# Seven products instead of eight in the last group's down projection, and product 4 of a job issued right behind its product 3

## The reference

```
def half_swiglu(x, g, w_gu, w_down):
    h = rmsnorm(x, g) @ w_gu                    # 1024 -> 2 x 2816
    a, b = jnp.split(h, 2, axis=-1)
    return x + 0.5 * ((jax.nn.silu(a) * b) @ w_down)   # 2816 -> 1024
...
for i in range(DEPTH):                          # DEPTH = 2
    h = half_swiglu(h, norm_ffn_a[i], w_ffn_a_gu[i], w_ffn_a_down[i])
    h = h + mixer(rmsnorm(h, norm_mix[i]))
    h = half_swiglu(h, norm_ffn_b[i], w_ffn_b_gu[i], w_ffn_b_down[i])
    h = h + sigmoid(rmsnorm(h, norm_ple[i]) @ ple_w_gate[i]) * (p[i] @ ple_w_proj[i])
```

## Time and profile before

| | us |
|---|---|
| median of 3 runs | 2784.4 (2784.36 to 2786.01) |
| the profiled execution | 2784.26 |
| its span, first to last instruction | 2782.7 |
| PE busy | 2744.7 (99%) |
| DVE busy | 1920.1 (69%) |
| ACT busy | 1207.2 (43%) |
| POOL busy | 191.7 (7%) |

### The profile page before, as it was taken

One profiled execution on the slowest core, in us unless ns is written; L12 is line 12 of the kernel. 1 busy time (PEld: TensorE's weight loads), 2 busy tenths in 40 slices (PEclk: granted clock), 3 DMA queues, 4 the chain that ended last, 5 costly groups with the idle time before them and its releaser, 6 DMA issues.

```text
span 2782.7 us, 47474 instructions
## 1 busy us (share of the span) xinstructions
PE 2744.7 (99%) x18946; PEld 2699.7 (97%) x18946; DVE 1920.1 (69%) x2691; ACT 1207.2 (43%) x1629; POOL 191.7 (7%) x190
## 2 busy tenths in 40 slices
PE   8999999999999999999999999999999999999997
PEld 8999999999999999999999999999999999999997
DVE  7888864646464678888557788865555568888755
ACT  5445443323132444454444455444534443545443
POOL 0000003101010110000010000002000020000021
PEclk9999999999999999999999999999999999999998
DMA  3322323333232313323321222223222112232231
GB/s 120 95 84 79 97 79 124 110 103 114 92 110 95 104 55 94 87 81 92 93 76 60 85 85 87 88 84 121 88 83 91 68 61 72 77 101 77 86 99 53
DMA packets 80909, 246.96 MB, mean 89 GB/s; under 512 B 8465, under 2 KB 25121, under 8 KB 79681
## 3 DMA queue, kind: packets, MB, share of 16 engines
q1 hardware_dynamic: 71408, 204.67, 23.6%
q0 software_dynamic: 9296, 39.40, 3.9%
HBM read 226.74 MB, written 17.30 MB: 88 GB/s over the span
## 4 chain that ended last, share of the span: by engine, by line
PE 97%; DVE 2%; ACT 0%; issue 0%; DMA 0%; ACTq 0%; SPq 0%; DVEq 0%
PE ps L618 42%; PE ps L547 35%; PE ps L930 7%; PE ps L806 4%; PE ps L983 2%; PE ps L599 1%; PE ps L904 1%; PE ps L1017 1%; PE ps L967 1%; PE ps L871 1%; PE ps L855 0%; PE ps L1003 0%; PE ps L874 0%; PE ps L849 0%; PE ps L883 0%
## 5 line engine op out<-in xcount | busy, mean ns | idle before, releaser
L1086 ACT ACTIVATE w_hi<-raw 128x1024 fp32r<-128x1024 f32 (+2 forms) x210 | 201.3, 959 | 522.4 <-PE ps L547 382.3
L1729 DVE TENSOR_TENSOR w_lo<-raw,w_hi 128x1024 fp32r<-128x1024 f32 (+2 forms) x210 | 238.1, 1134 | 100.5 <-ACT w_hi L1086 97.5
L547 PE MATMUL ps<-x_hi,w_hi 128*128 128x320 f32 x1216 | 283.7, 315 | 9.7 <-DVE x_lo L1734 8.7
L547 PE MATMUL ps<-x_hi,w_lo 128*128 128x320 f32 x1216 | 277.6, 310 | 0.0
L547 PE MATMUL ps<-x_lo,w_hi 128*128 128x320 f32 x1216 | 277.4, 309 | 0.0
L547 PEld LDWEIGHTS ps<-x_hi,w_hi 128*128 128x128 f32 x1216 | 204.3, 188 | 13.5 <-DVE w_lo L2472 8.7
L547 PEld LDWEIGHTS ps<-x_lo,w_hi 128*128 128x128 f32 x1216 | 203.9, 188 | 0.0
L547 PEld LDWEIGHTS ps<-x_hi,w_lo 128*128 128x128 f32 x1216 | 203.7, 188 | 0.0
L1150 ACT ACTIVATE wx_hi<-raw 128x1024 fp32r<-128x1024 f32 (+1 forms) x92 | 92.4, 1004 | 252.4 <-PE ps L618 215.1
L618 PE MATMUL ps<-x_hi,w_hi 128*128 128x320 f32 x576 | 178.7, 310 | 0.0
L618 PE MATMUL ps<-x_hi,w_lo 128*128 128x320 f32 x576 | 177.9, 309 | 0.0
(11 more groups left out here) (310 smaller groups left out, 7714.4 us busy)
## 6 DMA issues: line engine op xcount, KB each, us to landing
raw<-wst SPq DMA_DIRECT2D x292, 512.0 KB, 3.6
raw<-wst SPq DMA_DIRECT2D x96, 384.0 KB, 3.2
raw<-wst SPq DMA_DIRECT2D x32, 256.0 KB, 2.6
s<-st_d POOLq DMA_DIRECT2D x8, 1024.0 KB, 5.1
sts_o<-s POOLq DMA_DIRECT2D x16, 512.0 KB, 3.3
rd<-dec_d POOLq DMA_DIRECT2D x8, 640.0 KB, 5.5
kc<-kc_d POOLq DMA_DIRECT2D x8, 512.0 KB, 4.3
vc<-vc_d POOLq DMA_DIRECT2D x8, 512.0 KB, 5.2
```

The lines of the kernel that those rows point to most:

```text
L547: last = nc.tensor.matmul(out[:, h, :], a, b[:, HALF * h:HALF * (h + 1)], start=start and q == 0, stop=stop and q == 2, skip_group_check=True)
L1086: nc.scalar.activation(w_hi[:, (c["n"] + m) % 2, 0:cols], raw[:, r, 0:cols], ACT.Copy).then_inc(s_whi, 1)
L1729: tt(w_lo[:, p, 0:cols], raw[:, r, 0:cols], w_hi[:, p, 0:cols].bitcast(F), ALU.subtract).then_inc(s_wlo, 1)
```

## The change

Three things are done at once.

1. `SEVEN_DOWN` gets group 3 too: its down projection becomes four dn jobs of seven products. The eight plain units go, `x_hi`, `x_lo` and the squares for the next phase are made two tiles at a time (`fed`, `square_of`), and the squares move to another place in SBUF (`squares`).
2. On PE, product 4 of the old job moves up behind its product 3: 1, 3 old, 4 old, 2, 6, 5, 7.
3. ACT's and DVE's orders in a job follow: `hi12(new)` and `lo12(new)` move behind the finished job's work.

```
-SEVEN_DOWN = (1, 2)
+SEVEN_DOWN = (1, 2, 3)
...
                             third(old)
-                            second().then_inc(s_prod[2], 1)
-                            sixth().then_inc(s_prod[6], 1)
                             if after_start:
                                 split_up_to("T4")
                             fourth(old)
+                            second().then_inc(s_prod[2], 1)
+                            sixth().then_inc(s_prod[6], 1)
                             fifth()
...
-                    with pe.Fori(0, KT // 4) as i:
-                        for j in range(4):
-                            step(m + j, i, 4)
-                            project(c, m + j, i, 4, (c["unit"] + 1 + m + j) % 4, [(k, k) for k in range(nf)],
-                                    tiles(g_hi), tiles(g_lo), ready if j == 0 else None)
...
+                def fed(d):
+
+                    act.wait_ge(s_up, CREDIT + 2 * d["sum"] + 2)
+                    feed_hi(c["norm"] + 1, d["out"])
+                    act.wait_ge(s_free, CREDIT + o + d["m"] + 2)
+                    feed_hi(c["norm"] + 1, d["out"] + 1)
+
+                def square_of(n):
+                    square(c["fed"] + KT, c["norm"] + 1, n, s_xhi, c["fed"] + KT + n + 1)
...
-                        elif new:
-                            hi12(new)
-                        if made and made["seven"]:
+                        if made:
                             silu(made)
-                            snap2(d)
-                        elif old:
-                            snap2(d)
-                            if made:
-                                silu(made)
                         hi34(d)
                         if made:
                             ghi(made)
+                        if old:
+                            if new:
+                                hi12(new)
+                            elif c["split_p"]:
+                                act.wait_ge(s_p, 16 * (c["ple"] + 1))
+                                nc.scalar.activation(p_hi[:], p_raw[:], ACT.Copy).then_inc(s_phi, 1)
+                            snap2(d)
+                        if piece == LAST and d["kind"] == "dn":
+                            fed(old)
+                            square_of(old["out"])
+                            square_of(old["out"] + 1)
...
                         if new:
                             s1_s2(new)
+                        if made:
+                            c12(made)
+                        if new:
                             s3(new)
+                        if made:
+                            gated(made, 1)
+                            if made["seven"] and made["odd"]:
+                                g_sum(made, 1)
+                            gated(made, 0)
+                            if made["seven"]:
+                                g_sum(made, 2)
+                        if new:
                             if old:
                                 lo12(new)
                             else:
                                 lo1(new)
                                 lo2(new)
-                        if made:
-                            c12(made)
-                            gated(made, 1)
...
                             s4(new)
                         lo34(d)
...
                     if piece == LAST:
-                        silu(d)
+                        fed(d)
                         split_hi(c, d["m"] + 1, 0, 0, c["fill"] + d["m"] + 2)
-                        ghi(d)
+                        square_of(d["out"])
+                        square_of(d["out"] + 1)
```

More of the change, by code:

```diff
@@ L254, in trunk @@
         with ExitStack() as s:
+            sb("over_t_hi2", [P, 3, 4, HALF], F, s)
+            sq_mix = sb("sq_mix", [P, 2, TOK], F, s)
+            sb("over_t_mid", [P, 3 * 4 * HALF - 4 * TOK], F, s)
+            sq_ple = sb("sq_ple", [P, 2, TOK], F, s)
+        with ExitStack() as s:
             sb("over_t2", [P, 2, 3, 4, HALF], F, s)
@@ L432, in b_side, with squares @@
             return quarter(whole, *at_x[product]) if product < 5 else extra[:, product - 5, :, :]
+        def squares(norm):
+            if norm == 0 or norm > len(phases) - 1 or phases[norm - 1] != "ffn":
+                return sq
+            return sq_ple if phases[norm] == "ple" else sq_mix
         def g_tile(buf, k):
@@ L1096, in square @@
                 act.wait_ge(s_ssum, CREDIT + c_fed + d - 1)
-                nc.scalar.activation(sq[:, d % 2, :], x[:, d, :], ACT.Square).then_inc(s_sq, 1)
+                nc.scalar.activation(squares(norm)[:, d % 2, :], x[:, d, :], ACT.Square).then_inc(s_sq, 1)
             def feed(c_fed, norm, d, s, value):
@@ L1312, in ffn @@
                     for d in range(KT):
-                        if nf_at < LAST and d >= KT - 2:
+                        if d >= KT - 2:
                             if d == KT - 2:
@@ L1598, in add_squares @@
                         pool.wait_ge(s_ss, CREDIT + norm)
-                        nc.gpsimd.tensor_copy(ssum[:], sq[:, 0, :]).then_inc(s_ssum, 1)
+                        nc.gpsimd.tensor_copy(ssum[:], squares(norm)[:, 0, :]).then_inc(s_ssum, 1)
                     else:
                         pool.wait_ge(s_ssum, CREDIT + fed + d)
-                        nc.gpsimd.tensor_tensor(ssum[:], ssum[:], sq[:, d % 2, :], ALU.add).then_inc(s_ssum, 1)
+                        nc.gpsimd.tensor_tensor(ssum[:], ssum[:], squares(norm)[:, d % 2, :], ALU.add).then_inc(s_ssum, 1)
             def ffn(c):
@@ L1963, in winograd @@
                             c11_c12(summed)
-                            s1_s2(new)
-                            s3(new)
                             c21(summed)
-                            lo12(new)
-                            s4(new)
+                            if new:
+                                s1_s2(new)
+                                s3(new)
+                                lo12(new)
+                                s4(new)
+                            elif c["split_p"]:
+                                dve.wait_ge(s_phi, CREDIT + c["ple"] + 1)
+                                tt(p_lo[:], p_raw[:], p_hi[:].bitcast(F), ALU.subtract).then_inc(s_plo, 1)
                             lo34(d)
+                            if piece == LAST and d["kind"] == "dn":
+                                feed_lo(c["fed"] + KT, c["norm"] + 1, summed["out"])
+                                feed_lo(c["fed"] + KT, c["norm"] + 1, summed["out"] + 1)
                             continue
@@ L1997, in winograd @@
                         split_lo(c, d["m"], 0, 0)
-                        c12(d)
-                        gated(d, 1)
-                        gated(d, 0)
+                        c11_c12(d)
+                        c21(d)
+                        feed_lo(c["fed"] + KT, c["norm"] + 1, d["out"])
+                        feed_lo(c["fed"] + KT, c["norm"] + 1, d["out"] + 1)
                         split_lo(c, d["m"] + 1, 0, 0)
-                        glo(d)
                 for nf_at, nf in enumerate(PIECES):
@@ L2062, in ffn @@
                             t_low((6, 1, 2, 3, 4)[d], 3 + d)
[L2063 to L2068, removed]
+                        if d == KT - 4:
                             first = fast_pairs(c, nf_at + 1)[0]
```

13 lines of the change are left out of this document (3 added, 10 removed).

## The result

The changed kernel took 2827.5 us (median of 4; 2823.8 to 2829.5) beside 2784.4 before: 1.0151 of it, with a 95% interval of 1.0136 to 1.0167, or **43 us more**. I had forecast +20 with a range that ended at 2822. The direction was right, the size was not.

The account below looks back on a forecast made before the run. PE, busy 99% of the span, was taken to bound the kernel, so only fewer matmuls or new gaps count. From 2784.3, -21.1 + 30.8 + 0.7 + 9.4 = +19.8 gave 2804 us, range 2785 to 2822.

Parts of the forecast that it names:

- The saving: Group 3's down projection: 252 matmuls in place of 288, 5.28 us less in each of four FFNs, -21.1 us.
- The ring: Fast groups' gu jobs: DVE's cycle of freeing a raw slot, loading and splitting outlasts PE's job, PE waits, +30.8 us.
- The even turn: Gu jobs, even finished job: s1 to next s1 takes 12.54 us, 0.22 over PE's job.
- The odd turn: Gu jobs, odd finished job: s1 to next s1 takes 13.76 us, 1.44 over PE's job, including 3.82 for the load.
- The final group's own jobs: Group 3's dn jobs: DVE's 9.2 us of work fits PE's 9.24, nothing taken, 1 us a group as bad end.
- The tail: Behind each FFN: two tiles end together, so PE waits for ssum in ple, ret and sb, +9.4 us (0 to 15).
- the first dn job: Final group: the 0.16 us wait at the first dn job comes once more in each FFN, +0.7 us.
- the rivals: Cycle fits PE's job: 2773, 11%; loads sooner: 2785, 8%; loads later: 2820, 10%; change not doing what it says: excluded.
- Loads land later, or the dn jobs of group 3 become DVE's: Rival: loads take 4.08 us or more, 47 for 30.8, giving 2820, or DVE bounds group 3's dn jobs, 2824; 10%.

Follow-up runs that it names:

- after_lo34: The changed kernel with DVE's lo34(d) moved ahead of lo12(new) and s4(new) in gu jobs behind a gu job: 2795.8 us, 1.0042 of before.
- seven_only: The kernel before with only group 3's seven products added; product order and ACT's and DVE's gu orders as before: 2798.6 us, 1.0053 of before.
- adds_later: The changed kernel, but POOL waits for both x_lo of a pair (first three pairs) before it adds the squares: 2819.6 us.

## Why the prediction was wrong

**The saving** of 21.1 us was right, by the count of matmuls.

**The ring** was right in size: its term was +30.8, and undoing it in the changed kernel gave back 31.7. In mechanism it was half right. The even turn was 12.26 for 12.54, by a load that took 3.57 there in place of 3.82. The odd turn came out at 13.76 to the hundredth, and that is luck: no load is waited for in it, and what closes it is DVE's own work behind `lo34`, which stood in no hop of mine and happens to be 3.85 us long.

**The final group's own jobs** is the step that failed: "By their widths DVE has some 9.2 us of work against PE's 9.24: I take nothing". The work was 9.17, but the third job took 12.75, since POOL's two additions in a row fell on it. I had taken the addition's 2.05 us as the whole price of POOL and DVE meeting, which is POOL's side of it. What DVE pays did not stand in the sum: before, each FFN tile had one addition in 5.28 us, beside a DVE that was idle for 2.6 of them, and the `x_lo` there started first and took 0.88. The rule that I named for the tail, from the Trainium skill, "SBUF — State Buffer", section "SBUF: two separate sides" (whichever of a DVE instruction with two SBUF inputs and a GpSimd instruction starts first has the shared ports for its whole length), the trace bears out: two `x_lo` take 4.27 us for 1.68 behind the start of an addition, an `x_lo` that starts ahead of one keeps its 0.88, and with an input from PSUM `c22` keeps its 0.48. I had applied it to the tail alone, and there it was said to add nothing.

**The tail** I had at +9.4, from waits of 3.2 in each `ple` and 1.5 in `ret` and `sb`. (The pieces that I listed add up to 8.9 us and not 8.5; with 8.9 the term would have been 11.0.) The rows give 2.8 in each `ple`, 1.3 in `ret`, and in `sb` a wait of 2.2 for `c21` (L1902), 1.3 more than before, in place of one for `ssum`: 8.2. The waits were right in size; what I lacked is the clock at 0.50 to 0.67 behind the long ones, in the tail and in the final group.

Counted in both traces from the start of one matmul of PE to the start of another, in us for all four FFNs:

| part | forecast | before | changed | difference |
|---|---|---|---|---|
| groups 1 to 3, their first 2016 matmuls in each FFN | +30.8 | 1185.6 | 1217.2 | +31.6 |
| final group's down projection, 288 matmuls, then 252 | -21.1 + 0.7 | 170.0 | 171.7 | +1.7 |
| the 200 matmuls behind it | +9.4 | 119.6 | 133.7 | +14.1 |
| all the rest | 0 | 1307.5 | 1303.5 | -4.0 |
| span | +19.8 | 2782.7 | 2826.1 | +43.4 |

So the final group lost 1.7 + 21.1 = 22.8 us where I had put 0.7, and that is most of what the forecast missed. It is also one of the signs of being wrong that I had named: the final group waits for DVE by more than a few us. The rows of waits name 10.3 for `c22`, 1.3 for `lo34`, 1.3 more than before for `c21` in front of `sb`, and 0.7 for the first dn job. Of the 11 us at the low clock some 6 lie in this part and some 5 in the 200 matmuls behind it. The rest of the kernel is the same code; most of its -4.0 is a single place in the first `ret`, where PE waited 2.9 us before and then ran 3.4 us at a granted clock of 0.50, and 0.6 us with no such fall in the changed kernel.

The runs agree in size. after_lo34, where the ring is out, lies 10.6 above the kernel before in spite of the saving, so final group and tail cost 31.7 there; seven_only gives 15.1 + 21.1 = 36.2.

Of the rivals none came true. "Loads land later, or the dn jobs of group 3 become DVE's" named the right place at 2820 and more, but by the load and by DVE's own work, and neither was the cause.

## What to carry to other kernels

When work moves so that two engines that share ports meet, price the meeting on both of them: GpSimd's additions, hidden before beside a VectorE that idled, cost 29 us where VectorE had no slack left; 7 came back by an earlier start in the tail. When an order is changed around a queue of loads, add up the whole turn from slot freed to slot freed with the rows of before, and beside the load add up the engine's own instructions of the same stretch: here they were as long as the load. Then look for the instruction that frees the slot, and for an idle place to put it in: one line moved gave back 22 and 32 us. And a wait of TensorE of some 3 us can cost half as much again behind it.

## What was not expected of the hardware

A held DVE instruction shows no idle time in the timeline: it starts on time and is longer (0.54 to 1.93 us for `lo7`). With two additions in a row POOL starts the second 0.17 us behind the first (the last row of adds_later), and the DVE instruction that stands next is held as well.

After a wait of 2.8 us TensorE's granted clock was 0.55 for the next 3.5 us in the second FFN, 0.61 over 4 us behind the wait of 2.9 in the fourth, and 1.00 after the same wait in the first. Why it fell in some and not in the other stays open.
